# Attention stage of a decoder layer on one core: values' two parts as one operand, scores on half the rows of the array, another order of VectorE's and ScalarE's work

## The reference, cut to what matters

```python
    qkv = u @ wqkv
    q = rmsnorm(q, gq)
    k = rmsnorm(k, gk)
    ...
    kb, vb = band(k), band(v)
    scores = jnp.einsum('bnqkgd,bnskd->bnkgqs', qb, kb).astype(jnp.float32) * (HD ** -0.5)
    ...
    scores = scores - slopes[:, :, None, None] * dist.astype(jnp.float32)
    scores = jnp.where(mask[None, :, None, None], scores, -jnp.inf)
    m = jnp.maximum(scores.max(axis=-1), sink)
    e = jnp.exp(scores - m[..., None])
    probs = e / (e.sum(axis=-1) + jnp.exp(sink - m))[..., None]
    o = jnp.einsum('bnkgqs,bnskd->bnqkgd', probs.astype(v.dtype), vb)
    return o.reshape(b, s, H * HD) @ wo
```

## Time and profile before

| | |
|---|---|
| median of 3 runs | 1110.06 us (1107.3 to 1110.34) |
| the profiled execution's own time | 1107.26 us |
| its span in the profile | 1105.50 us |
| TensorE busy | 1084.9 us (98%) |
| VectorE busy | 732.2 us (66%) |
| ScalarE busy | 429.8 us (39%) |
| GpSimd busy | 148.4 us (13%) |
| TensorE's granted clock | full in all 40 slices |

### The profile page before, as it was taken

One profiled execution on the slowest core, in us unless ns is written; L12 is line 12 of the kernel. 1 busy time (PEld: TensorE's weight loads), 2 busy tenths in 40 slices (PEclk: granted clock), 3 DMA queues, 4 the chain that ended last, 5 costly groups with the idle time before them and its releaser, 6 DMA issues.

```text
span 1105.5 us, 14894 instructions
## 1 busy us (share of the span) xinstructions
PE 1084.9 (98%) x5272; PEld 910.3 (82%) x5272; DVE 732.2 (66%) x1130; ACT 429.8 (39%) x776; POOL 148.4 (13%) x272
## 2 busy tenths in 40 slices
PE   7899999998999999999999999999999999999998
PEld 5788888887888888888888888888888888888886
...
GB/s 267 20 20 20 19 19 0 38 184 26 92 138 76 114 73 209 118 191 153 153 132 190 39 191 218 390 411 293 299 285 289 288 227 76 39 39 59 95 39 39
DMA packets 61361, 153.88 MB, mean 139 GB/s; under 512 B 4720, under 2 KB 5752, under 8 KB 61304
## 3 DMA queue, kind: packets, MB, share of 16 engines
...
...
q10 hardware_dynamic: 24, 0.01, 0.0%
...
## 4 chain that ended last, share of the span: by engine, by line
PE 90%; DVE 5%; issue 2%; ACT 1%; POOL 1%; ACTq 0%; DVEq 0%; POOLq 0%
PE pair L2204 24%; PE pair L2184 21%; PE pair L1919 10%; PE pair L2056 8%; PE pair L2247 8%; PE pair L2224 4%; PE pair L1990 4%; PE pair L2142 3%; PE pair L1958 2%; PE pair L2260 2%; PE pair L2112 1%; PE pair L1969 1%; PE pair L1943 1%; PE pair L1901 0%; DVE RES L1722 0%
## 5 line engine op out<-in xcount | busy, mean ns | idle before, releaser
L2204 PE MATMUL pair<-uT 128*128 128x512 f32 x1176 | 266.7, 389 | 0.0
L2204 PEld LDWEIGHTS pair<-uT 128*128 128x128 f32 x1176 | 220.7, 188 | 45.8
L1193 ACT ACTIVATE uT<-wo_raw 128x1024 fp32r<-128x1024 f32 x63 | 64.4, 1054 | 104.9 <-PE pair L2204 90.4
L1919 PE MATMUL pair<-WA,xT 128*128 128x512 f32 x384 | 95.9, 398 | 5.3 <-DVE WA L1292 3.8
L1735 DVE TENSOR_TENSOR uT<-wo_raw,uT 128x1024 fp32r<-128x1024 f32 x63 | 74.9, 1221 | 38.8 <-ACT uT L1193 38.7
L675 POOL TENSOR_SCALAR row_var<-row_ssq 128x1 f32<-128x1 f32 x16 | 3.0, 191 | 700.3 <-ACT hn L1092 700.3
L2056 PE MATMUL pair<-WA,oT 128*128 128x512 f32 x384 | 90.3, 392 | 2.6 <-DVE WA L1491 2.1
L1919 PEld LDWEIGHTS pair<-WA,xT 128*128 128x128 f32 x384 | 69.6, 188 | 22.4 <-issue 6.8
L2056 PEld LDWEIGHTS pair<-WA,oT 128*128 128x128 f32 x384 | 71.2, 188 | 17.5 <-issue 3.1
L2184 PE MATMUL pair<-WA,WB 128*128 128x512 f32 x336 | 78.2, 389 | 0.4 <-ACT xr L1168 0.4
L2184 PEld LDWEIGHTS pair<-WA,WB 128*128 128x128 f32 x336 | 63.0, 188 | 13.8 <-DVE WB L1669 0.8
...
## 6 DMA issues: line engine op xcount, KB each, us to landing
...
```

Source lines behind the costliest of these rows:

```text
L1193: nc.scalar.activation(operand(t, which, HI), unit(t, which), ACT.Copy).then_inc(op_hi, 1)
L1919: mm = nc.tensor.matmul(proj_bank[X][:], xT[:, s, kt, :], w[:, m, kt, at:at + BANK], start=(kt == 0 and i == 0), stop=(kt == KT - 1 and i ...
L2204: mm = nc.tensor.matmul(ps[4 * (j % 2) + m][:], operand(t, 0, s)[:, k, m * P:(m + 1) * P], operand(t, 1, r)[:, k, :], start=(g == 0 and k ...
```

## The change

It does the following, all in the attention stage:

- `vz` becomes `[P, 2, KV, 2, HD]`: high and low part of a value head side by side, without zeros, so its memset goes. `weigh_values` is now 2 x 2 matmuls of 512 columns: weights high and low (64 + 64 columns), moving data all 4 heads' probabilities. The product's rows 0 to 63 are the output by the high value part, rows 64 to 127 that by the low one, for all heads.
- `attention_out` on ScalarE evicts that whole product in four copies of 64 rows x 256 columns, two to `RES` and two to a new `low_out`; `add_lows` on VectorE adds the two, one stage later than the copies (lag 3), and `attended` is now told by it, `pv_copied` by the copies.
- `qT` becomes `[P, 2, H // 2, P]`: even heads on rows 0 to 63, odd heads on 64 to 127, high and low apart. `scores` is now three passes x two head pairs x two row halves, 12 matmuls of 64 rows and 256 columns, where the two of a pair write to different banks; one `scores_ready` per group, one `copy_predicated` of 128x512. Both head gains are folded into the key's (`g_both`), so q is one copy and one subtraction of 128 rows.
- Order on VectorE: merge, `add_lows`, bias; `head_sums("q8")` behind the bias; `head_scale("q0")` ahead of `head_sums("k")`; `head_scale("k")` behind `scale_probs`; `v_diff` in group 1. Order on ScalarE: `pT_hi_part` ahead of `attention_out`, `part_squares("k")` ahead of `exps`; at the end `attention_out(30)` behind `oT_hi_half(1, 1)`.

The diff, without renamed semaphores and the counts of waits that follow from the above:

```diff
--- before.py
+++ after.py
...
@@ -144,10 +144,12 @@
         xT = sb("xT", [P, 2, KT, P], F32R, in_a)
         kn = sb("kn", [P, 2 * KV * HD], F32, in_a)
         qn = sb("qn", [P, H * HD], F32, in_a)
-        qT = sb("qT", [P, H, P], F32R, in_a)
+        qT = sb("qT", [P, 2, H // 2, P], F32R, in_a)
         kT = sb("kT", [P, 2, KV, 2, P], F32R, in_a)
         vnext = sb("vnext", [P, KV * HD], F32, in_a)
-        vz = sb("vz", [P, 2, 2, (2 * KV + 1) * HD], F32R, in_a)
+        vz = sb("vz", [P, 2, KV, 2, HD], F32R, in_a)
+        low_out = sb("low_out", [P, 2, 2 * P], F32, in_a)
+        sb("after_low_out", [P, 768], F32, in_a)
...
@@ -951,8 +942,14 @@
                 act.wait_ge(w_split, U_W1)
                 act.wait_ge(pv_done, t + 1)
+                wait(act, attended, t - 1)
                 dst = RES[:].rearrange("p b n -> p (b n)")[:, bass.ds(n * D + j * 2 * P, 2 * P)]
-                nc.scalar.activation(dst, pv_bank[:, 0:2 * P], ACT.Copy).then_inc(attended, 1)
+                nc.scalar.activation(dst[0:HD, :], pv_bank[0:HD, 0:2 * P], ACT.Copy)
+                nc.scalar.activation(low_out[HD:P, j % 2, :], pv_bank[HD:P, 2 * P:4 * P], ACT.Copy)
+                nc.scalar.activation(low_out[0:HD, j % 2, :], pv_bank[HD:P, 0:2 * P], ACT.Copy)
+                nc.scalar.activation(dst[HD:P, :], pv_bank[0:HD, 2 * P:4 * P], ACT.Copy).then_inc(pv_copied, 1)
             def before(n, j, lag):
...
@@ -992,26 +988,25 @@
                             xT_hi_half(n + 1, 0)
                             xT_hi_half(n + 1, 1)
                     if j == 3 and not last:
-                        q_hi_part("q0", n + 1, 0)
-                        q_hi_part("q0", n + 1, 1)
+                        q_hi_part("q0", n + 1)
                     if last:
                         last_part(n, j)
                         continue
                     if j == 1:
-                        q_hi_part("q8", n, 0)
-                        q_hi_part("q8", n, 1)
+                        q_hi_part("q8", n)
+                    if j == 2 and not last:
+                        part_squares("k", n + 1)
                     exps(n, j)
                     if j == 1 and not last:
                         part_squares("q0", n + 1)
                     if j == 2 and not last:
-                        part_squares("k", n + 1)
                         stage_v(n + 1)
                     if j == 3 and not last:
                         k_hi_part(n + 1)
+                    if not (first and j < 1):
+                        pT_hi_part(t - 1, (j - 1) % 2)
                     if not (first and j < 2):
                         attention_out(*before(n, j, 2))
-                    if not (first and j < 1):
-                        pT_hi_part(t - 1, (j - 1) % 2)
                     if j == 1:
                         v_hi_part(n)
                     if j == 0 and not last:
...
@@ -1067,16 +1062,15 @@
             part_squares("q0", 0)
             hi_unit(10, "q8", 2)
             hi_unit(11, "q8", 3)
-            q_hi_part("q0", 0, 0)
-            q_hi_part("q0", 0, 1)
+            q_hi_part("q0", 0)
             body(0, first=True)
             with act.Fori(1, NB - 2) as n:
                 body(n)
             body(NB - 2)
             body(NB - 1, last=True)
-            attention_out(NB - 1, GROUPS - 2)
             pT_hi_part(NB * GROUPS - 1, 1)
             oT_hi_half(1, 1)
+            attention_out(NB - 1, GROUPS - 2)
             oT_hi_half(2, 0)
             attention_out(NB - 1, GROUPS - 1)
             oT_hi_half(2, 1)
...
@@ -1334,46 +1328,51 @@
...
-            def q_lo_part(X, b, odd):
-                high, low = q_rows(odd, HI), q_rows(odd, LO)
-                dve.wait_ge(T_hi[X], 2 * b + (1 + odd))
-                nc.vector.scalar_tensor_tensor(
-                    out=qT[low, q_heads(X, odd), :], in0=turn_bank[X][high, :].rearrange("p (a n) -> p a n", a=G),
-                    scalar=gq_s[high, :], in1=qT[high, q_heads(X, odd), :].bitcast(F32), op0=ALU.mult,
-                    op1=ALU.subtract).then_inc(T_ready[X], 1)
+            def q_lo_part(X, b):
+                dve.wait_ge(T_hi[X], b + 1)
+                nc.vector.tensor_tensor(qT[:, LO, q_pairs(X), :], turn_bank[X].rearrange("p (a n) -> p a n", a=G),
+                                        qT[:, HI, q_pairs(X), :].bitcast(F32), ALU.subtract).then_inc(T_ready[X], 1)
+            def add_lows(n, j):
+                dve.wait_ge(pv_copied, 4 * n + (j + 1))
+                dst = RES[:].rearrange("p b n -> p (b n)")[:, bass.ds(n * D + j * 2 * P, 2 * P)]
+                nc.vector.tensor_tensor(dst, dst, low_out[:, j % 2, :], ALU.add).then_inc(attended, 1)
+            def before(n, j, lag):
+                return (n, j - lag) if j >= lag else (n - 1, j - lag + GROUPS)
...
-            def add_bias(n, j, first):
-                t, i = 4 * n + j, j % 2
+                nc.vector.tensor_tensor(vz[:, 0, :, LO, :], vprev[:].rearrange("p (v d) -> p v d", v=KV),
+                                        vz[:, 0, :, HI, :].bitcast(F32), ALU.subtract).then_inc(v_ready, 1)
+            def merge_scores(n, j, first):
+                t = 4 * n + j
                 if first:
                     dve.wait_ge(current_ready, 2)
-                for half_bank in range(2):
-                    stand(dve, scores_ready, 2 * t + (1 + half_bank))
-                    nc.vector.copy_predicated(score_keys[half_bank][:, :, 0, :],
-                                              current[:].bitcast(U32).unsqueeze(1).to_broadcast([P, 2, P]),
-                                              score_keys[half_bank][:, :, 1, :]).then_inc(wrapped, 1)
+                stand(dve, scores_ready, t + 1)
+                nc.vector.copy_predicated(score_keys[:, :, 0, :],
+                                          current[:].bitcast(U32).unsqueeze(1).to_broadcast([P, G, P]),
+                                          score_keys[:, :, 1, :]).then_inc(wrapped, 1)
+            def add_bias(n, j, first):
+                t, i = 4 * n + j, j % 2
                 for r in range(G):
                     if r == 0:
                         if first:
...
@@ -1412,33 +1410,29 @@
             def last_part(n, j):
                 t = 4 * n + j
+                merge_scores(n, j, False)
+                add_lows(*before(n, j, 3))
+                add_bias(n, j, False)
                 if j == 0:
                     head_sums("q8", n)
-                    add_bias(n, j, False)
                     wo_lo_unit(0)
                     head_scale("q8", n)
                     wo_lo_unit(1)
-                    pT_lo_part(t - 1, (j - 1) % 2)
                     v_diff(n)
                 if j == 1:
-                    q_lo_part("q8", n, 0)
-                    q_lo_part("q8", n, 1)
-                    add_bias(n, j, False)
-                    pT_lo_part(t - 1, (j - 1) % 2)
-                    v_lo_part(n)
+                    q_lo_part("q8", n)
                     wo_lo_unit(2)
-                    wo_lo_unit(3)
                 if j == 2:
-                    add_bias(n, j, False)
                     oT_lo_half(1, 0)
-                    pT_lo_part(t - 1, (j - 1) % 2)
                     wo_lo_unit(4)
                 if j == 3:
-                    add_bias(n, j, False)
-                    pT_lo_part(t - 1, (j - 1) % 2)
                     wo_lo_unit(5)
+                pT_lo_part(t - 1, (j - 1) % 2)
                 invert(n, j)
                 scale_probs(n, j)
+                if j == 1:
+                    v_lo_part(n)
+                    wo_lo_unit(3)
                 if j == 3:
                     wo_lo_unit(6)
                     wo_lo_unit(7)
...
@@ -1449,38 +1443,36 @@
                     if last:
                         last_part(n, j)
                         continue
+                    merge_scores(n, j, first)
+                    if not (first and j < 3):
+                        add_lows(*before(n, j, 3))
+                    add_bias(n, j, first)
                     if j == 0:
                         head_sums("q8", n)
-                    add_bias(n, j, first)
-                    if j == 0:
-                        if not last:
-                            xT_lo_half(n + 1, 0)
-                            xT_lo_half(n + 1, 1)
+                        xT_lo_half(n + 1, 0)
+                        xT_lo_half(n + 1, 1)
                         head_scale("q8", n)
                     if j == 1:
-                        q_lo_part("q8", n, 0)
-                        q_lo_part("q8", n, 1)
+                        q_lo_part("q8", n)
+                        v_diff(n)
                     if j == 2:
                         if isinstance(n, int) and n == NB - 2:
                             oT_lo_half(0, 0)
                             oT_lo_half(0, 1)
-                        if not last:
-                            head_sums("k", n + 1)
-                            head_scale("q0", n + 1)
```

(48 more changed lines are left out.)

92 lines of the change are left out of this document (40 added, 52 removed).

## The result

The changed kernel takes 1117.65 us (median of 6 runs, 1114.77 to 1118.79), the kernel before 1110.26 beside it (6 runs, 1107.30 to 1111.51). The ratio is 1.0066, 95% interval 1.0049 to 1.0084: 0.7% slower, clear of noise. I had forecast 1109.0. The profiled execution took 1116.61 us, of them 1114.8 span, so 9.3 more span than the one of before (1105.5). Of that difference some 2 us are the luck of the two executions: the profiled one of before lies 3.0 us under its median, that of the changed kernel 1.0. Of the 85 executions of the kernel before on record, the profiled one is among the 11 whose mean granted clock is 1.000 (spans of 1104.6 to 1105.7 us); the other 74 have 0.995 to 0.998 and 1106.2 to 1110.2 us, and no trace shows where they lose it.

A forecast was written before the change was run, and what follows sets the result against it. TensorE was taken to bound the kernel. From 1107.26 us, blocks 0 to 6 (-2.2 or +2.5) and the end (+1.1) gave 1106.2 or 1110.9, 1109.0 to 1113.7 on the median's footing; 1109 was taken, range 1096 to 1121.

The forecast's parts named there:

- Place A: From group 0's scores to the next block's q0 projection: 4.64 us becomes 5.01 (+0.37), VectorE binding; restart +0.25.
- Place B: From the end of k's projection to q8's projection: 3.33 us becomes 3.67 (+0.34), behind k's normalisation.
- The block: One block of 128 rows, 30.25 us before: -0.32 us, or +0.36 with the pipe emptied.
- the cover: Slack by which other engines' results precede TensorE's need: 0.36 us at Place A, none at Place B.
- Rival 2: The cover holds: 1086 us if neither place binds, 1101 or 1098 if only one is covered; chance 0.22.
- Scores: Twelve half-row matmuls a group: 0.71 us if pairs run together (-0.24), 1.43 one after the other (+0.48).
- the emptying of the pipe: Changing between 128-row and 64-row work on TensorE: at best nothing, at worst twice 0.17, 0.34 us a group.
- Block 7 "at 0": Block without projections, already waiting on VectorE and ScalarE (4.3 us of idle TensorE): the change was put at 0.
- The tail: At the end, group 30's eviction behind oT's copy delays the last value product: 1.70 us becomes 2.8, +1.1.
- the forecast case alone: Score pairs run together, Place A and Place B both bind: 1103 to 1115 us, chance 0.42.
- rival 1: Score weights load one by one, pairs gain nothing: +1.12 us a block, 1119, or 1124 with pipe emptied; chance 0.31.
- Rival 3: Added copies make ScalarE late for xT or k: 0.5 to 1 us a block, 1113 to 1117; chance 0.05.

The follow-up runs named there:

- experiment 12: The changed kernel with the old full-row scores (8 matmuls, q's old copies and subtractions, one merge), values and queues as changed: 1116.87 us, ratio 1.0063.
- experiment 4: The changed kernel with a bare eviction, one 128x256 copy and no addition, leaving part of the result out: 1109.38 us, ratio 0.9997.
- experiment 8: The kernel before with the values' part of the change alone, scores and all queue orders old: 1122.56 us, ratio 1.0109.
- experiment 13: The changed kernel with only ScalarE's queue of block 7 and of the tail in the old order: 1110.96 us, ratio 1.0007.
- experiment 5: The changed kernel with identity transposes (24, 22 and 18) filling TensorE's long waits in block 7: 1113.98 us, ratio 1.0044.

## Why the prediction was wrong

**What held.** The value matmuls are 4 a group in pieces of 0.92 to 0.94 us. Place A, walked at 5.01, is 127.82 - 122.75 = 5.07; it was 4.64. Place B, walked at 3.67, is 3.62 to 3.64; it was 3.33. Both have the releasers foretold, at 0.80 us idle each. The block, forecast between -0.32 and +0.36, is +0.08. So the step that matters most for the method is right: in blocks 1 to 6 each group has 0.52 us less TensorE work in the values, and there is no gain, since the cover was already gone. Rival 2, which let the cover hold, is refuted. Blocks 0 to 6 with what precedes them, forecast at -2.2 to +2.5, are -1.35. That is near the lower end by luck: I took block 0 to be like the others, and it alone gave 2.0 us, while blocks 1 to 6 cost 0.85.

**Scores: right range, wrong end.** I took 0.71 us a group. The pieces are 0.91 for 12, and an idle 0.17 us (ended by issue) stands ahead of them where the transposes end (142.72 + 0.36 to 143.25): 1.08 together. A pair takes 0.152, neither 0.119 (together) nor 0.238 (one by one). The 0.17 us is as large as the emptying of the pipe that I had from a duration of 0.29 less a pace of 0.119, and full-row scores have no idle time ahead of them (experiment 12). The Trainium skill (TensorEngine Tiling (Array Packing), Key Properties) says that a change of tiling mode drains TensorE; the trace agrees for the way in. Behind the scores it shows no idle time, but the next piece is longer: the 24 matmuls behind group 3's scores take 5.58 us to the next instruction (136.23 to 141.81), 5.47 before (108.17 to 113.64) and 5.47 in experiment 12. The part of the block between the two places should have lost 1.28 - 0.25 = 1.03 us; it lost 0.66 (30.33 - 5.07 - 3.64 = 21.62 against 22.28), and most of what is missing is the scores'.

**Block 7 "at 0": the step that failed.** It costs 7.0 us, 8.8 with the tail. I had seen that block 7 waits on VectorE and ScalarE already, and from that I put the change there at 0. This holds for work taken from TensorE. The other half was missing: where TensorE's wait ends with ScalarE, work added to ScalarE's queue ahead of that end lengthens the wait. The 0.8 us that I gave to each eviction (measured: 1.2 more, since the copies are paced 0.39 and not 0.28) I divided over 50 us of ScalarE's time and found room. In blocks 1 to 6 that was right (experiment 4: 0.05 us a block). In block 7 the single copy alone takes 6.5 us off the stretch, and ScalarE's old order with all four copies takes 6.4 off (some 1 of it the luck of the clock), so it is the two together: four copies, and their place.

**The order.** I wrote that the turned probabilities, copied ahead of the eviction, don't wait for it. True, and the new orders together are worth 1.2 us in a block of the loop (experiment 8 against 12; the share of this one was not tried). I did not ask the reverse: what now waits behind the turned probabilities. In block 7 it is the eviction and, behind it, the exponentials and the copy into `oT` (experiment 13).

**The tail.** Walked at +1.1. By the chain it went from 1.70 to 3.48 (288.02 to 291.50), so +1.8: the copies took 1.55 instead of 1.2, and the last value product 1.17 instead of 0.91. It is not the clock, which is 1.00 there; the product took 1.17 in experiment 5 too, behind the same wait, so the restart was missing from my sum. The mechanism was right, the size 0.7 short.

**The clock.** No step had it. Experiment 5 prices it at 3.0 us in the stretch and 1.6 behind it. The earlier trace rows showed TensorE idle 4.3 of 50 us there at a clock of 1.00, and I did not ask what more idle time would do to it.

In sum, on the profiled executions: forecast -1.1 to +3.6, of which I took the lower end; measured +9.3: -2.2 ahead of block 1's projection of q8, blocks 1 to 6 +0.85, the stretch without its tail +7.0, tail +1.8, behind it +1.8. By the medians the loss is 7.4. The time stayed inside the range of 1096 to 1121 by luck: it lies above the forecast case alone (1103 to 1115), and only rival 1, whose mechanism (scores one by one) did not happen, had stretched the range that far. Rival 3, copies that make ScalarE late, had 0.05 and 1113 to 1117; it had the right engine at the wrong place.
